# Prompt attention's query, key and value projections: one fp32 product against three f32r products of split operands

## The chip, the cores and the metric

The kernel runs on one core of one Trainium2 chip. The metric is the device time of one execution in microseconds. Each time of the kernel before is from the table below, or from one profiled execution on the same kind of core.

## The reference, cut to what matters

The kernel computes one layer of a hybrid decoder: a recurrence branch, a differential attention branch, a gated merge and a mixture of experts. What concerns us is the attention of the prompt. Its input is `xT`, the normed tokens (1024 channels, 1104 columns: 16 meta tokens, 64 sample tokens, 1024 prompt tokens).

```python
z = rmsnorm(x, norm1_w) @ w_in
hq, hf, hi, hg, dq, dk, dv, ga, gb = split_cols(z)
...
q_b = rmsnorm(dq.reshape(B, T, DA_HEADS, 2, DA_DH), q_norm_w)
k_b = rmsnorm(dk.reshape(B, T, DA_HEADS, 2, DA_DH), k_norm_w)
v_b = dv.reshape(B, T, DA_HEADS, DA_DV)
...
o_b = attn_core(q_b, k_b, v_b, lam)
```

`attn_core` takes per head two softmax maps with a relative bias, subtracts the second times `lam` from the first, and multiplies by the values. All data are float32. `k_b` and `v_b` are outputs too.

## The kernel before

The stages run one behind the other: norm and transposes, recurrence, attention of the prompt, merge (with the attention of the samples inside), output projection and routing, experts. The change lies in the attention stage, `phase_attention`.

That stage works head by head (4), and in each head tile by tile of tokens (9: one of 80 rows, eight of 128). A list of jobs, `slots`, is written out once, and each engine walks through it in its own program. Slot s (head s // 9, tile i = s % 9) has, in this order:

- `z`, the product of tile s+2: 8 steps over the channels, 384 columns (query, key, value of one head), into one PSUM bank (L972);
- `a`, turning the probabilities of slot s-1, one to three groups (L1017);
- the scores of slot s, two maps (L995, L997, in the last tile also L1006);
- `o`, probabilities times values of slot s-1 (L1031);
- `x`, turning query and key of tile s+1 (L981, L982), and `g`, turning the output of slot s-2 (L1039).

The list of one slot, as written:

```python
slot = make[s + AHEAD:s + AHEAD + 1]
...
    slot += [("a", s - 1, g) for g in range(groups(s - 1))]
...
    slot += [("L", s, 0), ("L", s, 1)] + ([("e", s, 0)] if s % NQ == NQ - 1 else [])
```

All jobs but the scores share four PSUM banks in turn (`bank_of`). `bank_free` makes TensorE wait until the job four places back has been read: for a bank that held a product that is the semaphore `normed`, which VectorE raises in `normalise` (L1205). With one group of `a` in a slot the job four places behind `z` is `g`; with two it is `x`; with three it is `o`.

Behind a product, ScalarE copies the values and squares query and key (`square`, L1065 and L1068). VectorE sums the squares (L1195), GpSimd takes the power, and VectorE scales (`normalise`, L1205, L1209). In one slot VectorE's order is: sum of squares, copy of turned probabilities (L928, L930, every second group; ScalarE copies the others at L1104), `maxima` of both maps (L1226, L1238: add the bias in PSUM, then reduce), `normalise`, `combine` (L1248 to L1254), scaling of an output (L1262). ScalarE's exponentials (L1095) stand between them.

Two buffers `Wb` hold the weights of two heads, loaded by SyncE's queue (L939). The keys and values of a head are stored when its last tile is through. Ahead of the first slot stand products 0 and 1 and the turning of tile 0, and the bias rows (L1044, L1122), which go to memory and come back skewed.

The merge stage behind it already multiplies split operands (tile `split`, L1438 to L1440, 368 columns): ScalarE rounds (L1515, L1521), VectorE subtracts the rounded part from the original (L1584, L1588).

Of the kernel before, what the change touches and what calls it, by code (L numbers as in the profile page):

```python
# [24 lines left out]
F32 = mybir.dt.float32  # L25
F32R = mybir.dt.float32r
I32 = mybir.dt.int32
ALU = mybir.AluOpType
# [27 lines left out]
SAMPLE = HEADS * DB * 32 + HEADS * FIRST + HEADS * P + KC * 256 + 2 * HEADS * 256  # L56
OUTPUT_SPLIT = 2 * KC * D + 4 * KC * P
# [78 lines left out]
def build(nc, A, out):  # L136
    with ExitStack() as stack:
# [42 lines left out]
        with nc.sbuf_tensor("sample_part", [P, SAMPLE], F32) as shared:  # L180
# [6 lines left out]
            with nc.sbuf_tensor("attention_part", [P, WORDS - start], F32) as rest:  # L187
                parts.append((rest, start, WORDS - start))
                phase_attention(nc, A, K, out, sb, psum, dram)
                parts.pop()  # L190
# [646 lines left out]
def phase_attention(nc, A, K, out, sb, psum, dram):  # L837

    W = A["w_in"][0].rearrange("(k p) n -> p k n", p=P)
# [33 lines left out]
    with ExitStack() as st:  # L873
        st.enter_context(nc.cleanup_on_exit())
        sem = lambda n: nc.alloc_semaphore(name="attention_" + n)
        w_in = [sem("w_in0"), sem("w_in1")]
# [6 lines left out]
        kv_out = [sem("kv_out0"), sem("kv_out1")]  # L883
# [8 lines left out]
        rel, rel31, relh, bucket, vecs = sb(HEADS), sb(HEADS), sb(HEADS, P), sb(ND), sb(HEADS, ND)  # L892
# [7 lines left out]
        def bank_of(job):  # L900
            return psum[:, 4 + turn_of[job] % 4, :]

# [31 lines left out]
        def _(sp):  # L934
            def weights(h):
                if h >= 2:
                    sp.wait_ge(projected, NT * (h - 1))
                for j, base in enumerate((DQ, DK, DV)):
                    sp.dma_start(Wb[h % 2][:, :, P * j:P * j + P], W[:, :, base + P * h:base + P * h + P]).then_inc(w_in[h % 2], 16)  # L939
# [5 lines left out]
            weights(1)  # L945
# [8 lines left out]
            for h in range(HEADS):  # L954
                sp.wait_ge(x_done, NT * (h + 1))
                for src, big, small in ((kout[h % 2], out["new_k_prompt"], out["new_k_sample"]),
                                        (v[h % 2], out["new_v_prompt"], out["new_v_sample"])):
                    sp.dma_start(big[0, 0, META:, h, :].rearrange("(i p) c -> p i c", p=P), src[:, 1:, :]).then_inc(kv_out[h % 2], 16)
                    sp.dma_start(big[0, 0, 0:META, h, :], src[0:META, 0, :]).then_inc(kv_out[h % 2], 16)
                    sp.dma_start(small[0, :, :, h, :].rearrange("b s c -> (b s) c"), src[META:FIRST, 0, :]).then_inc(kv_out[h % 2], 16)  # L960
                if h + 2 < HEADS:
                    weights(h + 2)
# [1336 lines left out]
```

## Time and profile before

| what | value |
|---|---|
| median of 3 runs | 1724.35 us (1719.77 to 1724.97) |
| the profiled execution's own time | 1728.1 us |
| its span | 1726.3 us |
| TensorE matmuls busy | 1547.2 us, 90% of the span |
| VectorE busy | 707.1 us, 41% |
| ScalarE busy | 461.9 us, 27% |
| GpSimd busy | 235.8 us, 14% |
| mean granted TensorE clock | 0.941 |

The span is the time between the first and the last instruction of the profile; it lies 1.8 us under the execution's own time. [...] An fp32 matmul has two records in the trace, so 8 of them show as x16.

### The profile page before, as it was taken

Reading aid. Unit: us, or ns where it says so; the run is one execution under the profiler, and the core shown is the slowest. Engines: PE = TensorE matmul, PEld = TensorE weight load, DVE = VectorE, ACT = ScalarE, POOL = GpSimd, SP = SyncE. Lnnn points to the kernel's source line nnn. Section 1 sums busy time; section 2 is a strip of 40 time slices with the busy share of each in tenths; the row PEclk is TensorE's granted clock in tenths of the full one; section 3 lists DMA queues with packets and bytes.
Section 4 is the critical chain, followed back from the end, with each engine's and each line's share of the span. In section 5 each row is a group of like instructions: output and inputs, shape, how many; then the busy total and the mean of one; then the engine's idle time right before and its main releaser. Section 6 shows DMA issues by size and latency. Waiting matters only on the chain. (4 is left out here: it accounts for less than half of the span.)

```text
span 1726.3 us, 22053 instructions
## 1 busy us (share of the span) xinstructions
PE 1547.2 (90%) x7497; PEld 1056.2 (61%) x7498; DVE 707.1 (41%) x1465; ACT 461.9 (27%) x1040; POOL 235.8 (14%) x417
## 2 busy tenths in 40 slices
PE   5999999986899898989789999999799929999996
PEld 3566565665465565655568888888678724444442
DVE  4368886886244453444432222233332241222121
ACT  2233343332233343334332222122232200111110
POOL 1000111011222222222100000000000001122221
PEclk8999999987799998989889999999999959999998
DMA  7001200000402001000055667233343392987973
GB/s 243 26 0 59 78 1 26 1 27 1 143 1 63 1 30 35 1 27 1 27 168 183 199 198 251 80 110 110 132 118 110 110 316 76 336 240 227 302 206 49
DMA packets 119369, 186.03 MB, mean 108 GB/s; under 512 B 9507, under 2 KB 82262, under 8 KB 117222
## 3 DMA queue, kind: packets, MB, share of 16 engines
q1 hardware_dynamic: 107750, 134.41, 24.4%
q0 software_dynamic: 11520, 50.34, 10.0%
q8 instruction: 57, 0.93, 0.2%
q14 instruction: 42, 0.34, 0.1%
HBM read 154.38 MB, written 30.34 MB: 107 GB/s over the span
## 5 line engine op out<-in xcount | busy, mean ns | idle before, releaser
L972 PE MATMUL psum<-attention_part,kept 128*128 128x384 f32 (+1 forms) x576 | 205.6, 513 | 0.7 <-DVE attention_part L1205 0.7
L2166 PE MATMUL psum<-moe_part,kept 128*128 x384 | 172.3, 602 | 6.4 <-issue 4.9
L972 PEld LDWEIGHTS psum<-attention_part,kept 128*128 128x128 f32 (+1 forms) x576 | 110.2, 196 | 78.7 <-issue 20.9
L1438 PE MATMUL psum<-split 128*128 128x368 f32 x384 | 140.6, 366 | 2.5 <-DVE split L1584 2.5
L498 PE MATMUL psum<-kept,recurrence_part 128*128 128x368 f32 x384 | 124.7, 480 | 10.0 <-PEq L236 5.0
L1427 PE MATMUL psum<-kept,sample_part 128*128 128x368 f32 x384 | 131.8, 487 | 1.3 <-PEq L873 1.3
L1440 PE MATMUL psum<-split 128*128 128x368 f32 x384 | 127.3, 332 | 0.0
L2166 PEld LDWEIGHTS psum<-moe_part,kept 128*128 128x128 f32 x384 | 72.3, 193 | 89.6 <-issue 89.6
L1439 PE MATMUL psum<-split 128*128 128x368 f32 x384 | 127.0, 331 | 0.0
L503 PE MATMUL psum<-recurrence_part,kept 128*128 128x512 f32 (+1 forms) x288 | 125.9, 593 | 0.0
L1593 DVE TENSOR_TENSOR merge_part<-merge_part,psum 128x368 f32<-128x368 f32 x48 | 25.8, 538 | 220.2 <-ACT merge_part L1527 220.2
L498 PEld LDWEIGHTS psum<-kept,recurrence_part 128*128 128x128 f32 x384 | 72.9, 194 | 54.3 <-issue 7.7
L1427 PEld LDWEIGHTS psum<-kept,sample_part 128*128 128x128 f32 x384 | 71.3, 192 | 41.3 <-issue 7.1
L1527 ACT ACTIVATE merge_part<-psum 128x368 f32<-128x368 f32 x48 | 22.9, 478 | 268.2 <-PE psum L1440 268.2
L503 PEld LDWEIGHTS psum<-recurrence_part,kept 128*128 128x128 f32 (+1 forms) x288 | 52.5, 186 | 64.1 <-issue 64.0
L2153 PE MATMUL psum<-moe_part,kept 128*128 x192 | 86.5, 593 | 1.1 <-ACT kept L2203 1.1
L518 PE MATMUL psum<-recurrence_part 128*128 128x128 f32 (+1 forms) x480 | 65.1, 292 | 21.4 <-DVE recurrence_part L806 21.4
L518 PEld LDWEIGHTS psum<-recurrence_part 128*128 128x128 f32 (+1 forms) x480 | 63.7, 207 | 33.0 <-issue 28.9
L2238 DVE TENSOR_TENSOR kept<-kept,psum 128x256 f32<-128x256 f32 x24 | 10.1, 421 | 168.3 <-ACT kept L2193 168.3
L1438 PEld LDWEIGHTS psum<-split 128*128 128x128 f32 x384 | 72.8, 190 | 9.2 <-DVE split L1584 3.6
L1031 PE MATMUL psum<-attention_part 128*128 128x128 f32 (+2 forms) x360 | 63.1, 321 | 15.7 <-DVE attention_part L1205 14.2
L1439 PEld LDWEIGHTS psum<-split 128*128 128x128 f32 x384 | 72.7, 189 | 5.6
(312 smaller groups left out, 2527.3 us busy)
## 6 DMA issues: line engine op xcount, KB each, us to landing
sample_part<-merge_gates POOLq DMA_DIRECT2D x16, 1024.0 KB
merge_part<-cache_kT SPq DMA_DIRECT2D x64, 256.0 KB, 3.4
merge_part<-cache_v SPq DMA_DIRECT2D x64, 256.0 KB, 3.1
moe_part<-w_gate SPq DMA_DIRECT2D x16, 1024.0 KB, 6.2
moe_part<-w_up SPq DMA_DIRECT2D x16, 1024.0 KB, 12.6
moe_part<-w_down SPq DMA_DIRECT2D x16, 1024.0 KB, 14.0
recurrence_part<-w_in SPq DMA_DIRECT2D x8, 1024.0 KB, 9.2
sample_part<-merge_out POOLq DMA_DIRECT2D x16, 512.0 KB, 6.4
```

What stands on the lines that cost most here:

```text
L498: mm = pe.matmul(bank[:, 0:CH], Wb[0][:, k, c0:c0 + P], K["xT"][:, k, CH * i:CH * i + CH], start=(k == 0), stop=(k == KC - 1))
L503: mm = pe.matmul(bank[:ROWS[i], :], K["xT"][:, k, cols(i)], Wb[1][:, k, :], start=(k == 0), stop=(k == KC - 1))
L518: pe.matmul(lev[:r, l - first, :r], Xu[:, l, xs], Xu[:, l, xs], start=True, stop=True)
L972: mm = pe.matmul(bank_of(("z", h, i))[:ROWS[i], 0:384], K["xT"][:, k, cols(i)], Wb[h % 2][:, k, :], start=(k == 0), stop=(k == KC - 1))
L1031: mm = pe.matmul(bank_of(("o", s, 0))[:r, 0:P], aT[:w, n, :r], v[h % 2][:w, 0 if n == i else n + 1, :], start=(n == 0), stop=(n == i))
L1427: mm = pe.matmul(bank_of(u, 2 * j), Wy[w % 2][:, k, P * j:P * j + P], src[:, k, chunk(n)], start=(k == 0), stop=(k == HEADS - 1))
L1438: pe.matmul(bank_of(u, 2 * j + 1), wh[w % 2][:, k, ch], xh[b][:, k, :], start=(k == 0), stop=False)
L1439: pe.matmul(bank_of(u, 2 * j + 1), wh[w % 2][:, k, ch], xl[b][:, k, :], start=False, stop=False)
L1440: mm = pe.matmul(bank_of(u, 2 * j + 1), wl[w % 2][:, k, ch], xh[b][:, k, :], start=False, stop=(k == KC - 1))
L1593: dve.tensor_tensor(b[:, j, :], b[:, j, :], bank_of(u, 2 * j), ALU.mult).then_inc(mixed, 1)
L2153: mm = pe.matmul(psum[:, 5 + n, :], hT[par][:, k, :], K["Wd"][:, bass.ds(2 * b + k, 1), 512 * n:512 * n + 512], start=(k == 0), stop=(k == 1))
L2166: mm = pe.matmul(psum[:, 2 + par, :], XT[par][:, k, :], K["GU"][:, bass.ds(KC * b + k, 1), :], start=(k == 0), stop=(k == KC - 1))
```

## The change

[...] Each operand is split into a rounded high part and the rest (`xh`, `xl`, `wh`, `wl`, all in a new tensor `attention_split`), and the product is high times high, high times low and low times high: 24 matmuls of 384 columns in place of 8.

```diff
+        view = lambda start, n: split[:, start:start + KC * n].rearrange("p (a b) -> p a b", b=n)
+        wh, wl, xh, xl = view(0, 384), view(KC * 384, 384), view(2 * KC * 384, P), view(2 * KC * 384 + KC * P, P)
-        Wb = [sb(KC, 384) for _ in range(2)]
+        Wb = sb(KC, 384)
...
-        kout = [sb(NT, P) for _ in range(2)]
+        kout = [sb(P) for _ in range(4)]
...
+        start = Pm.rearrange("p a b -> p (a b)")
+        vecs, bucket = start[:, 0:HEADS * ND].rearrange("p (a b) -> p a b", b=ND), start[:, HEADS * ND:HEADS * ND + ND]
+        relh = Am[:, 0:HEADS * P].rearrange("p (a b) -> p a b", b=P)
...
             def weights(h):
-                if h >= 2:
-                    sp.wait_ge(projected, NT * (h - 1))
-                for j, base in enumerate((DQ, DK, DV)):
-                    sp.dma_start(Wb[h % 2][:, :, P * j:P * j + P], W[:, :, base + P * h:base + P * h + P]).then_inc(w_in[h % 2], 16)
+                sp.wait_ge(w_split, 2 * h)
+                sp.dma_start(Wb.rearrange("p a b -> p (a b)"), A["attention_w"][h]).then_inc(w_in, 16)
...
             weights(0)
-            weights(1)
...
+                if h + 1 < HEADS:
+                    weights(h + 1)
+                for i in range(NT):
+                    n = NT * h + i
+                    sp.wait_ge(k_scaled, n + 1)
+                    if i:
+                        sp.dma_start(out["new_k_prompt"][0, 0, META + P * (i - 1):META + P * i, h, :], kout[n % 4]).then_inc(k_out[n % 4], 16)
...
             def product(h, i):
                 bank_free(pe, ("z", h, i))
-                pe.wait_ge(w_in[h % 2], 48 * (h // 2 + 1))
+                pe.wait_ge(x_split, NT * h + i + 1)
+                r, z = ROWS[i], bank_of(("z", h, i))[:ROWS[i], 0:384]
                 for k in range(KC):
-                    mm = pe.matmul(bank_of(("z", h, i))[:ROWS[i], 0:384], K["xT"][:, k, cols(i)], Wb[h % 2][:, k, :],
-                                   start=(k == 0), stop=(k == KC - 1))
+                    if i == 0 and k % 4 == 0:
+                        pe.wait_ge(w_split, 2 * h + k // 4 + 1)
+                    pe.matmul(z, xh[:, k, :r], wh[:, k, :], start=(k == 0), stop=False)
+                    pe.matmul(z, xh[:, k, :r], wl[:, k, :], start=False, stop=False)
+                    mm = pe.matmul(z, xl[:, k, :r], wh[:, k, :], start=False, stop=(k == KC - 1))
                 mm.then_inc(projected, 1)
...
+            def round_next(h, i):
+
+                n = NT * h + i + 1
+                if n < STEPS:
+                    act.wait_ge(projected, n)
+                    if n % NT == 0:
+                        round_w(n // NT)
+                    round_x(n)
+
+            def round_w(h):
+                act.wait_ge(w_in, 16 * h + 16)
+                for g in range(2):
+                    act.activation(wh[:, 4 * g:4 * g + 4, :], Wb[:, 4 * g:4 * g + 4, :], ACT.Copy).then_inc(w_rounded, 1)
+
+            def round_x(n):
+                act.activation(xh[:, :, :ROWS[n % NT]], K["xT"][:, :, cols(n % NT)], ACT.Copy).then_inc(x_rounded, 1)
+
+            round_x(0)
+            round_w(0)
...
                     elif kind == "z":
                         square(a, b)
+                        round_next(a, b)
...
-                if h >= 2:
-                    dve.wait_ge(kv_out[h % 2], 96 * (h // 2))
-                    dve.wait_ge(x_turned, NT * (h - 1))
+                if n >= 4:
+                    dve.wait_ge(k_out[n % 4], k_stored(n - 4))
...
+            def rest_next(h, i):
+                n = NT * h + i + 1
+                if n < STEPS:
+                    if n % NT == 0:
+                        rest_w(n // NT)
+                    rest_x(n)
+
+            def rest_w(h):
+                for g in range(2):
+                    part = slice(4 * g, 4 * g + 4)
+                    dve.wait_ge(w_rounded, 2 * h + g + 1)
+                    dve.tensor_tensor(wl[:, part, :], Wb[:, part, :], wh[:, part, :].bitcast(F32), ALU.subtract).then_inc(w_split, 1)
+
+            def rest_x(n):
+                dve.wait_ge(x_rounded, n + 1)
+                r = ROWS[n % NT]
+                dve.tensor_tensor(xl[:, :, :r], K["xT"][:, :, cols(n % NT)], xh[:, :, :r].bitcast(F32), ALU.subtract).then_inc(x_split, 1)
+
+            rest_x(0)
+            rest_w(0)
...
                     elif kind == "z":
                         sum_squares(a, b)
+                        rest_next(a, b)
```

There is one set of `xh` and `xl`, one of `wh` and `wl` and one `Wb`. To make room, the keys go out tile by tile from a ring of four, and the bias tables lie in the memory of the probabilities. The host lays the weights of one head out in one block (`attention_w`), so that one transfer brings them.

What the change moves on VectorE, in the slot of tile 2 of head 1. The rows before are sum of squares (L1195), the two maxima (L1226, L1238 each), then `normalise` (L1205, L1209):

```order
L1195 TENSOR_REDUCE attention_part<-attention_part 128x4
L1226 TENSOR_TENSOR psum<-psum,attention_part 128x256
L1238 TENSOR_REDUCE attention_part<-psum 128x1
L1226 TENSOR_TENSOR psum<-psum,attention_part 128x256
L1238 TENSOR_REDUCE attention_part<-psum 128x1
L1205 TENSOR_TENSOR attention_part<-psum,attention_part 128x256
```

The same place of the changed kernel, whose lines for these are L1238, L1268, L1280 and L1247; L1335 is the subtraction in `rest_x`:

```order
L1238 TENSOR_REDUCE attention_part<-attention_part 128x4
L1335 TENSOR_TENSOR attention_split<-kept,attention_split 128x1024
L1268 TENSOR_TENSOR psum<-psum,attention_part 128x256
L1280 TENSOR_REDUCE attention_part<-psum 128x1
L1268 TENSOR_TENSOR psum<-psum,attention_part 128x256
L1280 TENSOR_REDUCE attention_part<-psum 128x1
L1247 TENSOR_TENSOR attention_part<-psum,attention_part 128x256
```

One instruction of 1024 elements a partition stands between the sum of squares and the first maximum, and `normalise` follows behind both.

VectorE again, in the slot of tile 6 of head 1, whose product is the last of the head, before:

```order
L1195 TENSOR_REDUCE attention_part<-attention_part 128x4
L928 COPY attention_part<-psum 128x512
L1226 TENSOR_TENSOR psum<-psum,attention_part 128x256
L1238 TENSOR_REDUCE attention_part<-psum 128x1
L1226 TENSOR_TENSOR psum<-psum,attention_part 128x256
```

And in the changed kernel, where L1330 is the subtraction of half the weights of the next head (`rest_w`), and L937 the copy of turned probabilities:

```order
L1238 TENSOR_REDUCE attention_part<-attention_part 128x4
L1330 TENSOR_TENSOR attention_split<-attention_part,attention_split 128x1536 x2
L1335 TENSOR_TENSOR attention_split<-kept,attention_split 128x8x80
L937 COPY attention_part<-psum 128x512
L1268 TENSOR_TENSOR psum<-psum,attention_part 128x256
L1280 TENSOR_REDUCE attention_part<-psum 128x1
```

Two subtractions of weights and a short one of x stand ahead of the copy and the maxima here.

ScalarE at the slot of tile 2 of head 1, before: the values (L1065), the squares (L1068), then at once the exponentials (L1095):

```order
L1065 ACTIVATE attention_part<-psum 128x128
L1068 ACTIVATE attention_part<-psum 128x256
L1095 ACTIVATE attention_part<-psum,attention_part 128x272 x2
L1110 ACTIVATE attention_part<-psum,attention_part 128x128
L1080 ACTIVATE attention_part<-psum,kept 64x128 x2
```

And in the changed kernel, where L1154 is the rounding in `round_x`:

```order
L1084 ACTIVATE attention_part<-psum 128x128
L1087 ACTIVATE attention_part<-psum 128x256
L1154 ACTIVATE attention_split<-kept 128x1024
L1114 ACTIVATE attention_part<-psum,attention_part 128x272 x2
L1129 ACTIVATE attention_part<-psum,attention_part 128x128
```

The rounding stands between the squares and the exponentials.

## Rows read from the trace of the kernel before

**Rows 1.** The page, part 1: busy us (share of the span) x instructions.

```profile
PE 1547.2 (90%) x7497; PEld 1056.2 (61%) x7498; DVE 707.1 (41%) x1465; ACT 461.9 (27%) x1040; POOL 235.8 (14%) x417
```

**Rows 2.** TensorE in order of time, 604.9 to 615.7 us (start, us).

```profile
604.99 5.39 PE L972 MATMUL psum<-attention_part,kept 128*128 128x384 f32 x16
610.21 0.71 PE L1017 MATMUL psum<-kept,attention_part 128*128 128x128 f32 x5
...
615.30 0.30 PE L981 MATMUL psum<-kept,attention_part 128*128 128x128 f32 x1 [0.46 <-DVE attention_part L1205]
...
615.65 0.49 PE L972 MATMUL psum<-attention_part,kept 128*128 128x384 f32 x1
```

**Rows 3.** TensorE's waits, 449 to 830 us: total us, times, longest.

```profile
PE psum L1031 <- DVE attention_part L1205: 14.2, 6, 2.9
PE psum L1039 <- DVE attention_part L1205: 9.4, 15, 1.3
PE psum L981 <- DVE attention_part L1205: 3.8, 10, 0.5
```

**Rows 4.** TensorE in order of time, 581 to 585.65 us.

```profile
582.10 0.38 PE L1017 MATMUL psum<-kept,attention_part 128*128 128x128 f32 x2
...
585.49 0.20 PE L1039 MATMUL psum<-kept,attention_part 16*128 16x16 f32 x1 [0.69 <-DVE attention_part L1205]
```

**Rows 5.** VectorE in order of time, 582.5 to 585.5 us.

```profile
582.88 0.42 DVE L1195 TENSOR_REDUCE attention_part<-attention_part 128x4 f32<-128x256 f32 x1 [3.93 <-ACT attention_part L1068]
583.22 0.42 DVE L1226 TENSOR_TENSOR psum<-psum,attention_part 128x256 f32<-128x256 f32 x1
```

**Rows 6.** VectorE's waits, 449 to 830 us.

```profile
DVE psum L1226 <- PE psum L997: 7.2, 14, 0.7
...
DVE psum L1226 <- PE psum L995: 2.9, 3, 1.0
DVE attention_part L1234 <- PE psum L1006: 1.0, 3, 0.3
```

**Rows 7.** TensorE, 901.4 to 905.3 us: first and last of 23 matmuls.

```profile
901.47 0.33 PE L1439 MATMUL psum<-split 128*128 128x368 f32 x1
...
905.17 0.33 PE L1440 MATMUL psum<-split 128*128 128x368 f32 x1
```

**Rows 8.** VectorE's instructions on tile split: ns min/median/max.

```profile
L1588 DVE TENSOR_TENSOR split<-sample_part,split x16: 2291/2293/2294, 871.1 to 1218.1; 128x2048 fp32r<-128x2048 f32 x16
L1584 DVE TENSOR_TENSOR split<-kept,split x3: 3219/3225/3226, 873.6 to 1128.3; 128x2944 fp32r<-128x2944 f32 x3
```

**Rows 9.** ScalarE's instructions on tile split: ns min/median/max.

```profile
L1521 ACT ACTIVATE split<-sample_part x16: 1901/1902/1911, 869.1 to 1216.1; 128x2048 fp32r<-128x2048 f32 x16
L1515 ACT ACTIVATE split<-kept x3: 2640/2642/2671, 870.9 to 1125.5; 128x2944 fp32r<-128x2944 f32 x3
```

**Rows 10.** TensorE in order of time, 651 to 670.2 us.

```profile
651.75 3.03 PE L1031 MATMUL psum<-attention_part 128*128 128x128 f32 x16 [2.92 <-DVE attention_part L1205]
...
655.24 7.57 PE L972 MATMUL psum<-attention_part,kept 128*128 128x384 f32 x16
...
665.82 3.83 PE L1031 MATMUL psum<-attention_part 128*128 128x128 f32 x18 [1.83 <-DVE attention_part L1205]
```

**Rows 11.** Three stretches (length, busy us by engine, PEclk, DMA share).

```profile
653.00:659.00 6.00, 6.00 (x17) 3.82 (x16) 2.25 (x5) 2.73 (x8) 2.42 (x8) 0.50 0.02 5
667.00:670.00 3.00, 3.00 (x14) 2.55 (x13) 0.00 (x0) 0.27 (x2) 0.00 (x0) 0.50 0.00 0
671.00:700.00 29.00, 26.38 (x106) 16.63 (x105) 12.32 (x38) 11.25 (x41) 6.95 (x17) 1.00 0.00 0
```

**Rows 12.** A longer stretch, 550 to 652 us, the same columns.

```profile
550.00:652.00 102.00, 93.26 (x392) 60.97 (x393) 46.71 (x115) 38.61 (x127) 22.50 (x50) 0.95 0.10 28
```

**Rows 13.** TensorE in order of time, 442 to 456.1 us.

```profile
442.88 13.14 PE L972 MATMUL psum<-attention_part,kept 128*80 128x384 f32 x32
```

**Rows 14.** DMA issues, 425 to 475 us: count, KB each, us to landing.

```profile
attention_part<-w_in SPq DMA_DIRECT2D x6, 512.0 KB, 7.5
```

More of the change, by code:

```diff
@@ L186, in build @@
             assert top[0] == start
-            with nc.sbuf_tensor("attention_part", [P, WORDS - start], F32) as rest:
-                parts.append((rest, start, WORDS - start))
-                phase_attention(nc, A, K, out, sb, psum, dram)
+            with nc.sbuf_tensor("attention_split", [P, ATTENTION_SPLIT], F32R) as split, nc.sbuf_tensor("attention_part", [P, WORDS - start - ATTENTION_SPLIT], F32) as rest:
+                parts.append((rest, start + ATTENTION_SPLIT, WORDS - start - ATTENTION_SPLIT))
+                phase_attention(nc, A, K, out, sb, psum, dram, split)
                 parts.pop()
@@ L834, in _, with phase_attention @@
                     unit_gate(s // 3 + 2)
-def phase_attention(nc, A, K, out, sb, psum, dram):
-    W = A["w_in"][0].rearrange("(k p) n -> p k n", p=P)
+def phase_attention(nc, A, K, out, sb, psum, dram, split):
     NQ = NT
@@ L882, in phase_attention @@
             "logits", "max_done", "exp_done", "a_done", "a_turned", "a_act", "a_dve", "o_done", "ssq_done", "orstd_done", "og_done", "og_turned", "ob_done"))
-        kv_out = [sem("kv_out0"), sem("kv_out1")]
-        Wb = [sb(KC, 384) for _ in range(2)]
+        v_out, k_out = [sem(f"v_out{b}") for b in range(2)], [sem(f"k_out{b}") for b in range(4)]
+        view = lambda start, n: split[:, start:start + KC * n].rearrange("p (a b) -> p a b", b=n)
+        wh, wl, xh, xl = view(0, 384), view(KC * 384, 384), view(2 * KC * 384, P), view(2 * KC * 384 + KC * P, P)
+        Wb = sb(KC, 384)
         qz = [sb(2, TOK) for _ in range(2)]
         kT = [sb(TOK) for _ in range(2)]
-        kout = [sb(NT, P) for _ in range(2)]
+        kout = [sb(P) for _ in range(4)]
         v = [sb(NT, P) for _ in range(2)]
@@ L901, in bank_of, with k_stored @@
             return psum[:, 4 + turn_of[job] % 4, :]
+        def k_stored(n):
+            return 16 * sum(1 + (m % NT == 0) for m in range(n % 4, n + 1, 4))
         def bank_free(e, job):
@@ L981, in turn_qk @@
                 pe.transpose(bank[:, 0:r], zn[:r, n % 2, 0:P], K["ident"][:r, :r])
-                pe.transpose(bank[:, P:P + r], kout[h % 2][:r, i, :], K["ident"][:r, :r]).then_inc(x_turned, 1)
+                pe.transpose(bank[:, P:P + r], kout[n % 4][:r], K["ident"][:r, :r]).then_inc(x_turned, 1)
             def scores(s, m):
@@ L1123, in _ @@
             for kind, a, b in zx:
-                (square if kind == "z" else place_qk)(a, b)
+                if kind == "z":
+                    square(a, b)
+                    round_next(a, b)
+                else:
+                    place_qk(a, b)
             for s, slot in enumerate(slots):
@@ L2291 @@
     arrays["merge_gates"] = np.stack(branch_gate, axis=3).transpose(2, 1, 0, 3, 4).reshape(KC, P, -1).copy()
+    qkv = [arrays["w_in"][0, :, base:base + 512].reshape(KC, P, HEADS, P) for base in (DQ, DK, DV)]
+    arrays["attention_w"] = np.stack(qkv, axis=3).transpose(2, 1, 0, 3, 4).reshape(HEADS, P, -1).copy()
     arrays.update(constants())
```

31 lines of the change are left out of this document (18 added, 13 removed).

## The prediction

> **What bounds the kernel now.** I read the page first, to see whether TensorE is the engine to look at: it is busy 90% of the span [rows 1]. That is an average over stages, so I went to the attention stage (from about 443 us on), laid one slot out in order of time on TensorE, VectorE and ScalarE, and then asked for the waits. I number a slot by its query tile i (0 to 8) within its head, and call T the moment at which its product is over and L1017, the turning of probabilities, starts.
>
> In slot i=5 of head 1 the product starts at 604.99, T is 610.21, and the next product starts at 615.65 [rows 2]. So a product costs 5.22 us, and 5.44 us of other TensorE work and waiting follow. The reader is to see the 0.46 us idle before L981. TensorE there waits for `normed` (L1205), because the bank that it wants next is the one of this slot's product. This wait is not an accident of one slot: L1205 ends 31 waits of TensorE in this stretch, 27.4 us in all [rows 3]. So from T on the slot is set by VectorE's chain: sum of squares, a copy of turned probabilities in some slots, two biased maxima, then `normed`. The 5.22 us of product are set by TensorE. A slot is the sum of the two.
>
> **What the product gains.** The old product is 8 fp32 matmuls of 384 columns in 5.22 us. The new one is 24 matmuls of rounded operands. The same kind runs in the merge stage on 368 columns: from 901.47 to 905.17 there are 22 steps, 0.168 us each [rows 7]. Scaled to 384 columns by 384/368 that is 0.175, so 24 take 4.2 us: **1.04 us less** per product, 36 products, 37 us. A wait on top of it only matters behind these numbers.
>
> [...]
>
> **What the split costs.** Two conversions per product: ScalarE rounds 1024 elements a partition, VectorE subtracts. ScalarE took 1.902 us for 2048 and 2.642 for 2944 [rows 9], so 0.826 ns an element and 1.06 us for 1024. VectorE took 2.293 and 3.225 [rows 8], so 1.04 ns an element and 1.23 us for 1024. For half a head's weights (1536) it is 1.48 and 1.76. Together 57 us on VectorE (33 full x parts, 4 short ones, 8 half weights), 48 us on ScalarE: nothing against their load if it lay under the products. It does not. There is one `xh`, so rounding for product n+1 waits for `projected` of product n, and both engines do it at once, ahead of the slot's copies and maxima (the rows of the order in the section on the change). That is just the chain from T to `normed`.
>
> In time: in slot i=2, T is 582.10, and VectorE's sum of squares starts at 582.88, released by ScalarE's square (L1068), so that ends at about T+0.76 [rows 4, 5]; rounding then ends at T+1.8; the subtraction runs from T+1.84 to T+3.07. Without it VectorE is past its sum of squares at T+1.20 and starts the next work at T+1.12, since its neighbours overlap by some 0.08 [rows 4, 5]. So what follows starts **1.86 us later**. Slot i=2 shows the price bare: VectorE has no gap there, TensorE waits 0.69 us [rows 4], and 0.69 becomes 2.55. Where VectorE now waits for scores ahead of its maxima, that gap takes some of it. All such gaps of the stretch are 7.2 + 2.9 + 1.0 = 11.1 us [rows 6].
>
> The sum, at an unchanged clock:
> - 33 of the 34 slots with a product split for the next one: 33 x 1.86 = 61.4, less the gaps 11.1: **+50.3**.
> - Three of them (i=6 of heads 0 to 2) split the next head's weights first. ScalarE rounds from T+0.7 to T+3.6, VectorE subtracts until T+5.7, then 0.83 for the short x part: what follows starts 3.36 us later than with an x part alone: **+10.1**.
> - 34 products of 1.04: **-35.4**.
> - The opening. The weights of head 0 come at 7.5 us from issue [rows 14], as the first of six issues for two heads, and now in one transfer of 1.5 MB. I take them to be there about 1 us before the old first product began; rounding half of them (1.48) and subtracting it (1.76) then puts the first product near 445, against 442.88 [rows 13]. Products 1 and 2 each wait 3.2 us for their x part where they waited for nothing, and 3 waits 2.8. Against that stand 2 x 1.04, partly at half clock. I take **+8** for it.
> - The K output, now stored tile by tile, and its ring of four: each tile has three slots (about 30 us) to leave, on a queue that carries little here. Put at 0; that it costs under 2 us is bounded by 36 stores of 64 KB behind which only other stores and the next weights stand, and those are issued a head ahead.
> - The aliased bias tables are read before the first slot: 0.
>
> That is +33 us.
>
> **What the longer waits do to the clock.** Twice per head TensorE now idles long enough to be slowed. [...] The product at 655.24 took 7.57 instead of some 5.4. [...] The waits are now 1.83, 1.3, 0.7, 0.7, 0.3, 0.46, 0.4, 0.3 and 2.9 us for i = 0 to 8; with the chain 1.86 us longer less the gaps they become about 3.7, 3.1, 2.6, 2.6, 1.7, 2.1, 5, 1.6 and 3.5. So seven of nine slots are at or above the wait of 1.83 that was followed by a drop. I price a drop by half of its length, as the rows have them: 1.7 us where it lasts 3.4 (i=2, 3, 5), 3.4 where it lasts 6.8 (i=0, 1, 6, 8). That is 18.7 a head against 5.1 now (0.05 of 102 us [rows 12]); heads 1 and 2 lose 13.6 more, head 0 about 8.5, head 3, which has fewer products, 10: **+46** if every such wait brings its drop. Bounds: 0 from below (no more drops than now); from above all products at the lower level, 36 x 4.2 = 150, less the 20 paid now. I take three quarters of the 46, since a slot that runs slow leaves less idle time behind it: **+34**.
>
> So 33 + 34 = 67 us on the profiled execution's 1728.1: 1795. That execution lies 3.75 us (0.2%) over the median of the runs shown, and I forecast **1793 us**, slower by 4%.
>
> **The rivals.**
> - *The chain is longer, the clock as now.* The f32r products keep TensorE warm enough that waits of 2 to 3 us bring no more drops. For it: slot i=1's 1.30 us brought none [rows 3]; against it the 1.83 at 665.82. Time: 1724 + 33 = 1757, range 1745 to 1770. Chance 0.22.
> - *Slow for most of the stage.* Each drop runs into the next wait; the upper bound above, at two thirds: 1724 + 33 + 87 = 1844. For it: two drops lie only some 8 us apart [rows 10, 11]. Chance 0.08.
> - *Faster: the split is hidden.* One mechanism: if what follows `normed` were not waited for, because TensorE reaches its bank wait later than VectorE, the 37 us of products stay and only the opening and the three weight splits (18) are paid: 1724 - 37 + 18 = 1705. It decides from a chain that grows by less than 1.04 us per slot instead of 1.86 less the gaps (1.5 on average). For it: the waits on L981 are short, 0.5 us at most. Against it: they exist in 31 places, so hardly any slack is left on TensorE's side [rows 3]. Chance 0.07.
> - *No change beyond 0.3%*: the chain grows by about 1.2 us per slot and the clock stays. Chance 0.03.
>
> My forecast (chain longer, clock lower more often) has 0.60, with 1772 to 1825 as its own range. The overall range goes down to the first rival's low part and up to 1835, which leaves out the faster cases, the slowest one, and edges: 1748 to 1835. A measurement of this kernel can tell about 0.3% (5 us) from no change. Faster 0.07, same 0.03, slower 0.90.
>
> **What the changed profile would show.** Products: 24 matmuls in 4.2 us at full clock; if they take 5 us, the step of 0.175 is wrong. Rounding 1.06 and subtracting 1.23 us each, ending near T+3.1. TensorE's waits for `normed` in this stretch: 27 us now, near 75 to 90 us then, most of it before the turned output (L1039's line) and before L981's. A mean granted clock of 0.80 to 0.88 between 450 and 830 us, where it is 0.95 in head 1's stretch now [rows 12]; if it stays there, the first rival holds. A wait of 5 us in slot i=6 of heads 0 to 2. The merge stage and later: unchanged. I am wrong if the maxima can start before the subtraction is over, if ScalarE's rounding is much shorter than 1.06 us, or if the lower clock covers mostly the scores, which VectorE's chain hides.

## The result and the profile after

The changed kernel takes **1782.22 us** (median of 4 runs, 1779.48 to 1785.34) where the kernel before takes 1724.66 in the same session (1719.77 to 1726.35): a ratio of 1.0345, interval 1.0319 to 1.037. It is slower by 57.6 us. A few executions took far longer than the others of the same kernel; they are left out of the ratios here. Its profiled execution took 1784.34 us with a span of 1782.5, against 1726.3 before. The span's 56.2 us more lie here: the first product starts 4.4 us later (447.26 against 442.88 [rows 13]), from there to the end of the last product it takes 431.3 us against 382.1 (49.2 more), and what follows takes 2.6 more. Of the 4.4 at the start 2.4 are none of the change's: the bias products ahead of the stage already began that much later.

Part 1 of the page of the changed kernel:

```profile
PE 1547.7 (87%) x7785; PEld 1135.2 (64%) x7786; DVE 760.2 (43%) x1509; ACT 504.6 (28%) x1084; POOL 237.4 (13%) x417
```

VectorE has 53 us more work and ScalarE 43 [rows 1]. TensorE's busy time has not moved, though its products need less of it. The first place to look is again slot i=5 of head 1. TensorE in order of time (start, us):

```profile
634.50 0.41 PE L990 MATMUL psum<-attention_split 128*128 128x384 f32 x1
...
638.77 0.71 PE L1036 MATMUL psum<-kept,attention_part 128*128 128x128 f32 x5
...
642.58 1.54 PE L1050 MATMUL psum<-attention_part 128*128 128x128 f32 x10 [0.59 <-DVE attention_part L937]
645.31 0.30 PE L1000 MATMUL psum<-kept,attention_part 128*128 128x128 f32 x1 [1.19 <-DVE attention_part L1247]
...
645.63 0.41 PE L990 MATMUL psum<-attention_split 128*128 128x384 f32 x1
```

The product is 4.27 us long (638.77 less 634.50) where it was 5.22: 24 float32r matmuls of one record and 0.178 us each in place of 8 of two records and 0.65 us each. These are lengths from start to start; a matmul's own record overlaps the next one's (0.41 us against the step of 0.178). What follows is 6.86 where it was 5.44 [rows 2]. What the product gives, the rest of the slot takes and more. Slot i=2 of head 1 shows by which work. VectorE in order of time; T is 605.02 here:

```profile
605.81 0.42 DVE L1238 TENSOR_REDUCE attention_part<-attention_part 128x4 f32<-128x256 f32 x1 [4.54 <-ACT attention_part L1087]
606.75 1.23 DVE L1335 TENSOR_TENSOR attention_split<-kept,attention_split 128x1024 fp32r<-128x1024 f32 x1 [0.52 <-ACT attention_split L1154]
607.89 0.43 DVE L1268 TENSOR_TENSOR psum<-psum,attention_part 128x256 f32<-128x256 f32 x1
...
609.60 0.41 DVE L1247 TENSOR_TENSOR attention_part<-psum,attention_part 128x256 f32<-128x256 f32 x1
```

The first maximum starts at T+2.87, where it was T+1.12 [rows 4, 5]: 1.75 us later. Before the subtraction VectorE waits for the rounding, 0.52 us. ScalarE in the same slot:

```profile
605.39 0.38 ACT L1087 ACTIVATE attention_part<-psum 128x256 f32<-128x256 f32 x1
605.66 1.06 ACT L1154 ACTIVATE attention_split<-kept 128x1024 fp32r<-128x1024 f32 x1
```

TensorE's waits of the stage, 440 to 900 us (total us, times, longest):

```profile
PE psum L1050 <- DVE attention_part L939: 20.2, 10, 3.2
PE psum L1050 <- DVE attention_part L1247: 19.5, 6, 3.5
PE psum L1058 <- DVE attention_part L1247: 17.2, 15, 2.2
PE psum L1000 <- DVE attention_part L1247: 9.1, 10, 1.2
PE psum L990 <- DVE attention_split L1335: 8.3, 3, 3.0
...
PE psum L1050 <- DVE attention_part L937: 4.6, 3, 3.4
```

L1050, L1058 and L1000 are the outputs, the turned output and the turn of queries and keys, L1031, L1039 and L981 before. L1247 (`normed`) now ends 45.8 us of waits in these three rows where it ended 27.4 [rows 3]. The new rows are L939 and L937, VectorE's copies of the turned probabilities: 24.8 us. They stand behind the subtraction in VectorE's order, and the outputs of the slot need them.

The clock, by two stretches of the profile after (length, busy us by engine, PEclk, DMA share):

```profile
450.00:830.00 380.00, 303.98 (x1506) 261.63 (x1505) 191.26 (x418) 157.69 (x434) 78.03 (x168) 0.87 0.09 29
...
550.00:652.00 102.00, 84.40 (x440) 72.36 (x439) 50.81 (x115) 43.54 (x125) 22.53 (x49) 0.91 0.08 27
```

Over 450 to 830 us the mean granted clock is 0.87 (it was 0.95 in the same stretch before). From the first product to the last, TensorE stood at a granted clock of 0.50 for 115.1 us, against 42.8 before, by the trace's records of that clock, which hold only 1.00 and 0.50; I call this the half-clock time below, and 0.50 the lower level. A product that met the lower level took up to 7.16 us instead of 4.25.

So three things have to be told apart: the shorter product, the longer chain, and the clock.

### The profile page after: what moved, and what is told of

The parts are those of the page before. It is cut to its first block and busy times, and to the rows that moved or that the text cites. A ratio compares the mean times of both kernels' runs of the same rounds, so it can differ in the third digit from the quotient of the medians.

```text
span 1782.5 us, 22725 instructions
## 1 busy us (share of the span) xinstructions
PE 1547.7 (87%) x7785; PEld 1135.2 (64%) x7786; DVE 760.2 (43%) x1509; ACT 504.6 (28%) x1084; POOL 237.4 (13%) x417
## 5 line engine op out<-in xcount | busy, mean ns | idle before, releaser
L990 PE MATMUL psum<-attention_split 128*128 128x384 f32 (+1 forms) x288 | 116.7, 405 | 12.4 <-DVE attention_split L1335 8.3
L991 PE MATMUL psum<-attention_split 128*128 128x384 f32 (+1 forms) x288 | 111.9, 389 | 0.0
L992 PE MATMUL psum<-attention_split 128*128 128x384 f32 (+1 forms) x288 | 111.8, 388 | 0.0
L1050 PE MATMUL psum<-attention_part 128*128 128x128 f32 (+2 forms) x360 | 66.7, 335 | 47.6 <-DVE attention_part L939 20.2
L499 PEld LDWEIGHTS psum<-kept,recurrence_part 128*128 128x128 f32 x384 | 73.1, 194 | 54.5 <-issue 8.1
L1050 PEld LDWEIGHTS psum<-attention_part 128*128 128x128 f32 (+2 forms) x360 | 54.7, 225 | 54.8 <-issue 31.6
```

What stands on the lines that cost most here:

```text
L499: mm = pe.matmul(bank[:, 0:CH], Wb[0][:, k, c0:c0 + P], K["xT"][:, k, CH * i:CH * i + CH], start=(k == 0), stop=(k == KC - 1))
L990: pe.matmul(z, xh[:, k, :r], wh[:, k, :], start=(k == 0), stop=False)
L991: pe.matmul(z, xh[:, k, :r], wl[:, k, :], start=False, stop=False)
L1050: mm = pe.matmul(bank_of(("o", s, 0))[:r, 0:P], aT[:w, n, :r], v[h % 2][:w, 0 if n == i else n + 1, :], start=(n == 0), stop=(n == i))
```

## The experiments

Each session had its own runs of the kernel before, and ratios are against these. Figures of the stage run from the start of the first product to the end of the last.

**1. The splitting of x off the chain.** `xh` and `xl` get a second buffer each, so the parts for tile n+2 can be made at the end of a slot, when both engines have done what TensorE waits for. To make room, the ring of keys and the two work tiles of the norm move into the memory of the merge gates (`Wg_raw`), whose load then starts later. The weights' split stays where it was.

```diff
-        wh, wl, xh, xl = view(0, 384), view(KC * 384, 384), view(2 * KC * 384, P), view(2 * KC * 384 + KC * P, P)
+        wh, wl = view(0, 384), view(KC * 384, 384)
+        xh, xl = ([view(2 * KC * 384 + (2 * b + part) * KC * P, P) for b in range(2)] for part in range(2))
...
                 if 1 <= s <= STEPS:
                     scale_out(s - 1)
+                rest_x(s + 4)
```

> The changed kernel with two sets of xh and xl, so that the x part of tile n+2 is rounded and subtracted at the end of slot n, while TensorE multiplies, and not between projected and the maxima. The weights' split stays where it is. To make room, four small tiles lie in the merge stage's first weight buffer, whose load then comes at the end of the attention stage. My theory (the loss is the x part on VectorE's chain, and the lower clock behind the longer waits): the chain in all slots without a weight split is back to the one before, the products keep 4.25 us, so 1725 - 36 x 1.0 + 3 x 3.6 for the weight splits + 4 for the opening = 1704, within 1697 to 1712, and TensorE's clock in the stage near 0.93. Rival, the three f32r products with their many matmuls are what costs (by the clock or by the operand reads): it stays above 1760.

Measured: **1703.1 us**, ratio 0.9889 (0.9862 to 0.9917): faster than the kernel before by 1.1%, and the theory's 1704 was met. The same work on the same engines, at another place, is worth 79 us. TensorE in slot i=2 of head 1 (T is 568.92; L1061 is the turned output, L1258 `normalise`):

```profile
568.92 0.38 PE L1039 MATMUL psum<-kept,attention_part 128*128 128x128 f32 x2
...
572.31 0.20 PE L1061 MATMUL psum<-kept,attention_part 16*128 16x16 f32 x1 [0.69 <-DVE sample_part L1258]
572.44 0.44 PE L993 MATMUL psum<-attention_split 128*128 128x384 f32 x1
```

The wait is back at the 0.69 us of [rows 4], and half-clock time at 42.3 us.

**2. Only the subtraction behind `normalise`.** VectorE's order alone is changed; there is still one buffer, and ScalarE's rounding stays in its place.

```diff
                     elif kind == "z":
                         sum_squares(a, b)
-                        rest_next(a, b)
...
                 for kind, a, b in slot:
                     if kind == "z":
                         normalise(a, b)
+                        rest_next(a, b)
```

> The changed kernel with one thing moved: on VectorE the subtractions for the next product stand behind normalise of this one, ahead of combine, not ahead of the copies and maxima. Nothing is saved in work. My theory: VectorE no longer waits 0.65 us for ScalarE's rounding and its old gaps ahead of the maxima are used again, but TensorE's next product now waits for the subtraction itself: per head 4 us less, 16 in all, so 1766 (1758 to 1775). Rival, the split's place doesn't matter and only the clock or the products count: 1782 within 5.

Measured: **1776.7 us**, ratio 1.0322 (1.0297 to 1.0347). The theory said 16 us less, 1758 to 1775; the medians are 5.5 us apart, and the interval overlaps that of the changed kernel (1.0319 to 1.037), so the times don't show that anything was won. The waits show what happened. TensorE's, 440 to 900 us:

```profile
PE psum L990 <- DVE attention_split L1335: 49.5, 29, 5.9
PE psum L1050 <- DVE attention_part L1247: 14.0, 6, 2.9
PE psum L1058 <- DVE attention_part L1247: 7.0, 13, 1.0
```

The wait for `normed` is 24.1 us (with 3.1 ahead of L1000), nearly what it was before the change, and the next product waits for the subtraction instead, 29 times. With one buffer the next product cannot start before rounding and subtraction are over, wherever VectorE puts them. Another order around the one buffer moves the wait; the second buffer took it away.

**3. The split with the old product.** The kernel before, with x rounded and subtracted at the changed kernel's places into a result that nobody uses. The product waits for the subtraction as in the changed kernel, but it is the fp32 one.

```diff
                 pe.wait_ge(w_in[h % 2], 48 * (h // 2 + 1))
+                pe.wait_ge(x_split, NT * h + i + 1)
...
                     elif kind == "z":
                         square(a, b)
+                        round_next(a, b)
...
                     elif kind == "z":
                         sum_squares(a, b)
+                        rest_next(a, b)
```

> The kernel before with its fp32 products, and beside them the x part's rounding and subtraction at the very places where the change has them, with the same waits; their result isn't used, and the weights aren't split. My theory: the chain is longer by 1.75 us in 34 slots less some 11 us of gaps, 3 us twice in the opening, and a lower clock behind the longer waits, 10 to 20 us: 1725 + 48 + 6 + 15 = 1794 (1780 to 1810), so slower than the changed kernel although its products are the old ones. Rival, the cost of the change lies in the f32r products, the weights or the stores: 1725 to 1735.

Measured: **1801.69 us**, ratio 1.0473 (1.0437 to 1.0508), within what was expected. The split of x costs 79 us on its own, with no float32r matmul in the kernel. That is more than the whole loss: float32r products, in place of the fp32 ones, bring it down by some 20 us (19.5 between the medians, 21.4 when each is taken against its own session's kernel before), with the weights' split that they need paid from it.

**4. The other edits.** K stored tile by tile from a ring of four, the aliased bias tables and the weights in one block, with fp32 products and no split.

```diff
-        kout = [sb(NT, P) for _ in range(2)]
+        kout = [sb(P) for _ in range(4)]
...
+                sp.dma_start(Wb[h % 2].rearrange("p a b -> p (a b)"), A["attention_w"][h]).then_inc(w_in[h % 2], 16)
```

> The kernel before with the change's other edits alone: keys stored tile by tile from a ring of four, the bias tables in the memory of the probabilities, the weights in one contiguous transfer per head (two buffers kept), and fp32 products without any split. My theory: no effect, 1725 within 5. Rival, the 36 single stores on SyncE's queue or the waits for them cost part of the 57 us: 1735 or more.

Measured: 1722.58 us, ratio 0.9993 (0.9972 to 1.0013). They cost nothing that can be told from zero; the interval allows 2 us more or 5 less.

**5. TensorE kept busy in its waits.** This is to price the clock apart from the chain. Ahead of an instruction that was seen waiting, TensorE runs fp32 products of 128 by 128, about 0.22 us each, into columns of a bank that nobody reads then, counted out per slot to fill 85% of the wait of the trace. Their results are used by nobody. Where that bank isn't free yet, they wait for it first. The other engines' programs are not changed.

```diff
+            def keep_busy(s, kind):
+                n = count[kind][s]
...
+                for _ in range(n):
+                    pe.matmul(bank[:, 384:512], K["xT"][:, 0, 0:P], K["xT"][:, 1, 0:P], start=True, stop=True)
...
                 for kind, a, b in slot:
+                    if kind in "oxg":
+                        keep_busy(s, kind)
                     run[kind](a, b)
```

It was done to the changed kernel:

> The changed kernel with nothing else changed than this: where TensorE stood waiting in the attention slots (ahead of the outputs, of the turns of queries and keys and of the turned output), it first runs fp32 products of 128 by 128 into columns of a bank that nobody reads, 256 of them in all, about 0.22 us each, counted out per slot to fill 85% of the wait that the trace showed there. Their results are used by nobody. Theory (the waits bring the clock down, and the clock costs what the lengthened products cost): time at half clock from the first product to the last falls from 115 us to under 40, products stay at 4.25 us in nearly all slots, and of the 33 us by which 34 products exceed 4.25 us in the changed kernel some 25 go: 1757 us (1745 to 1766). Rival 1 (the falls do not hang on the waits): 115 us at half clock as before, 1782 plus what the added products delay (1782 to 1795). Rival 2 (a product at half clock is hidden by the chain of the other engines): half-clock time goes, the time stays at 1778 to 1784.

to the kernel before:

> The kernel before with the same filling of TensorE's waits, 103 products of 128 by 128. It tells whether the clock has a price in the kernel before too: of 12 us by which its 34 products exceed 5.2 us, some 8 to 10 go: 1716 us (1708 to 1722), half-clock time in the stage from 43 to under 20 us. If the falls do not hang on the waits: 1722 to 1730.

and to the kernel of experiment 1:

> The kernel with two split buffers for x (x_ring_of_two) with the same filling of TensorE's waits, 127 products of 128 by 128. Half-clock time in the stage 42 us to under 20, the excess of 10.6 us in the products mostly gone: 1695 us (1689 to 1702). If the clock has no price there: 1701 to 1706.

| kernel | as it is | waits filled | stage, us | half-clock time, us |
|---|---|---|---|---|
| before | 1724.66 | 1715.73 | 382.1 to 368.0 | 42.8 to 8.9 |
| changed | 1782.22 | 1744.23 | 431.3 to 398.7 | 115.1 to 27.6 |
| ring of two | 1703.1 | 1689.75 | 352.7 to 338.2 | 42.3 to 4.2 |

The ratios to the kernel before are 1.0121 (1.0073 to 1.0168) for the changed kernel with filled waits, 0.9953 (0.9935 to 0.997) for the kernel before with them and 0.9807 (0.9766 to 0.9847) for the ring. The ring and the kernel before came out as expected. With 256 useless products added, the changed kernel is 38 us faster. That is 0.8 us below the range that the theory gave, and neither rival stands: the falls of the clock hang on the waits, and they cost time. Of its 27.6 us of half clock that are left, 20.8 lie in the opening (from the first product to 482.29 us), where only two products were added. Two slots show it. First slot i=8 of head 0 of the changed kernel, TensorE in order of time:

```profile
567.22 3.60 PE L1014 MATMUL psum<-attention_part 128*128 128x512 f32 x8
570.66 0.51 PE L1025 MATMUL psum<-attention_part 128*128 128x16 f32 x4
574.32 2.24 PE L1050 MATMUL psum<-attention_part 128*128 128x128 f32 x16 [3.15 <-DVE attention_part L1247]
```

The same with filled waits, where L1088 are the added products:

```profile
560.23 0.52 PE L1025 MATMUL psum<-attention_part 128*128 128x16 f32 x4
560.59 2.92 PE L1088 MATMUL psum<-kept 128*128 128x128 f32 x24
563.89 2.24 PE L1050 MATMUL psum<-attention_part 128*128 128x128 f32 x16 [0.37 <-DVE attention_part L1270]
```

Twelve products (two records each) fill the wait of 3.15 us down to 0.37, and the outputs start as long after L1025 as before, 3.66 us. The next slot, i=0 of head 1, shows the gain. Its outputs in the changed kernel:

```profile
585.67 4.03 PE L1050 MATMUL psum<-attention_part 128*128 128x128 f32 x18 [3.30 <-DVE attention_part L1247]
```

and with the wait filled:

```profile
572.84 2.94 PE L1088 MATMUL psum<-kept 128*128 128x128 f32 x24 [0.90 <-ACT attention_part L1146]
575.62 2.36 PE L1050 MATMUL psum<-attention_part 128*128 128x128 f32 x18
```

The same 18 records take 2.36 us instead of 4.03. In the changed kernel a stretch at the lower level begins at 586.2 us, inside these outputs. The windows 550 to 652 and 652 to 755 us of the changed kernel with filled waits:

```profile
550.00:652.00 102.00, 97.05 (x605) 84.03 (x606) 58.37 (x125) 47.98 (x136) 23.18 (x50) 1.00 0.08 27
652.00:755.00 103.00, 97.60 (x607) 85.20 (x606) 57.98 (x126) 48.71 (x133) 23.12 (x50) 0.98 0.04 12
```

One blemish: in the kernel before, one wait was overfilled (slot i=8 of head 1, whose next product came at T+12.05 against T+10.13 and T+10.23 in the other heads), so that kernel could be some 1.9 us faster.

**6. Which waits do it.** The same filling of the changed kernel, once in the nine waits of 3.1 to 3.5 us alone, once in all others (2.2 us and less):

> The changed kernel with products of 128 by 128 put only into its nine waits of 3.1 to 3.5 us (ahead of the outputs of i = 6 of the slot loop's turn, i = 8 and the first of the next head, in each head's round), 109 of them. Theory (each fall follows a wait shortly ahead of it, and costs what it lengthens): the falls that stood behind these waits in the changed kernel (at 545.3, 586.2, 657.9, 685.2, 702.3 and 774.0 us, 34 us of half clock in all) go, those of the short slots (from 600, 716 and 815 us on) stay: half-clock time in the stage from 115 to 75 to 90 us, 1767 us (1761 to 1774). Rival (the clock answers to the stage's busy time as a whole): falls thin out everywhere, above all in the short slots too.

> The changed kernel with the products put into the other waits only, of 0.3 to 2.2 us each, 147 of them. By the theory the falls of the short slots go (those that begin at 600, 610, 620, 716, 726, 740, 815, 829, 839 and 849 us), those behind the long waits stay: half-clock time 115 to 50 to 70 us, 1761 us (1755 to 1769). Together the two savings should come near the 38 us that filling all waits gave. Rival (only waits of about 3 us and more bring the clock down, and the short slots' falls are their late echo): half-clock time stays above 100 and the time at 1778 to 1785.

Measured: 1765.29 us (ratio 1.0274, 1.0231 to 1.0318) with the long ones filled, 1758.08 (1.0232, 1.0192 to 1.0271) with the others. The kernel before, run beside these two, took 1718.11 us, 6.5 less than beside the changed kernel, so the medians can't be set against 1782.22 as they stand. Over the kernel before the two are 47.2 and 40.0 us slower, where the changed kernel was 57.6: 10.4 and 17.6 us saved, together 28, against 37.9 with all waits filled. The expectation that the two savings add up to the whole is neither shown nor refuted, as each interval is some 7 us either way. Half-clock time fell to 61.9 and 65.9 us. For the long ones that is more than expected (75 to 90), but part of it is not the added products' doing: in the opening, which has at most two of them, it was 7.4 and 7.9 us, against 26.3 in the changed kernel. (The fall at 815 us, which the expectations count with the short waits, stands behind a wait of 3.30 us.) The products show it slot by slot, from the middle of head 0 into head 1. With the long waits filled, the products of the slots i=2, 3 and 4 of head 1 took 6.70, 5.86 and 6.71 us, and those behind the filled waits of i=8 and i=0 4.26 and 4.34. With the others filled it is the reverse: 4.27, 4.29 and 4.26 in slots i=2 to 4, 6.00 behind the wait in i=6 and 6.30 behind that in i=8. So each kind of wait brings its own falls. With the long ones filled, all but one of the lengthened products behind the opening lie in the slots i=2 to 4. Ahead of each stands a wait of 1.6 to 2.2 us in slot i=1, 2 or 3, one in each slot of 9 to 12 us.

**7. The weights' split off the chain too.** On top of experiment 1, ScalarE rounds the next head's weights behind its copies, and VectorE subtracts behind `normalise`.

```diff
                     elif kind == "z":
                         square(a, b)
+                for kind, a, b in slot:
+                    if kind == "z":
                         round_next(a, b)
                 if s < STEPS:
                     exps(s)
...
                         sum_squares(a, b)
-                        rest_next(a, b)
...
                         normalise(a, b)
+                        rest_next(a, b)
```

> The kernel with two split buffers for x, and the split of the next head's weights taken off the chain as well: ScalarE rounds them after its copy of the turned probabilities and ahead of the exponentials, VectorE subtracts after it has normalised. In the slots of the split (i = 6, three of them, 9.8 us from product to product's start against about 6) first maxima come some 3.5 us sooner; ScalarE's rounding (about 2.8 us) still stands ahead of the exponentials. About 7 us less from the chain and up to 4 from the clock: 1692 us (1687 to 1700). Rival: the rounding delays the exponentials by as much as the subtraction delayed the maxima, so that the slot is as long as it was: 1700 to 1706.

Measured: 1699.6 us, ratio 0.9847 (0.9797 to 0.9897). The three slots i=6 became 12.05 us long in the mean instead of 14.1, 6 us in all, but the interval overlaps that of the ring, 0.9862 to 0.9917, so the times don't tell it. The same with TensorE's waits filled as well:

> Two split buffers for x, the weights' split off the chain, and TensorE's waits filled with 106 products. The ring with filled waits took 1689.8 us; taking the weights' split off the chain made three slots 1.7 us shorter each in the trace: 1685 us (1679 to 1691). Rival (the weights' split gives nothing more, since VectorE's subtraction then delays the next product): 1688 to 1692.

Measured: 1682.7 and 1683.3 us, with no ratio from so few, so the same kernel ran again:

> The kernel of ring_weights_kept_busy once more (88 added products, not the 106 that its expectation gave), since only two of its four executions were undisturbed, at 1682.7 and 1683.3 us. 1683 us (1680 to 1689), which puts it 5 to 7 us below the ring with filled waits and the weights' split left on the chain, and 2.0 to 2.4% below the kernel before. If the two executions were a lucky draw of the clock: 1687 to 1692.

Measured: **1685.0 us** (1682.92 to 1686.8, 6 runs), ratio 0.9778 (0.9753 to 0.9803), against 0.9807 (0.9766 to 0.9847) for the ring with filled waits. It is the fastest version found, 2.2% below the kernel before. That the weights' part of it is a gain is not shown by the times here either, since the intervals overlap; what shows it is the length of the three slots. What is left of the weights' split is in the waits of the first of these two runs, 440 to 785 us:

```profile
PE psum L993 <- DVE attention_split L1365: 5.2, 4, 1.5
PE psum L1061 <- DVE sample_part L1283: 3.3, 13, 0.4
```

L993 belongs to the product, L1365 is the subtraction of weights: the first product of each of the three next heads waits 1.5 us, in place of the 3.5 us by which the split had delayed `normed` (`normalise` of slot i=6 ended at T+9.07 in heads 0 and 2 of the ring, now at T+5.60).

## Why the prediction was right, and where its terms were off

The forecast was +69 us on the median, the measured change is +57.6, in the range and in the likeliest case: the chain longer and the clock lower. Its steps in their order:

- **The product, 1.04 us less.** Measured 4.24 to 4.27 against 5.22 at the full clock, 0.96 less, 32.7 us for 34 products at full clock against the 35.4 of the sum. The step measured on 368 columns held nearly: 24 steps from 634.50 to 638.77 are 0.178 us each, where 0.175 was forecast.
- **What follows starts 1.86 us later.** Measured 1.75, and 1.06 and 1.23 us for the two conversions as forecast. The start of the subtraction (T+1.73 against T+1.84) is what was off.
- **The gaps, and +50.3.** With the waits filled in both kernels, so that the clock hardly speaks, the 28 slots from the third on that split no weights are 37 us longer outside their products (the overfilled one set right), 1.32 each; the sum had 1.52. In slots i=1 to 3 the 1.75 came through nearly whole (1.5 to 1.9), in i=7 it was 0.6 to 0.7 and in i=8 0.2 to 0.3. There VectorE waited 0.65 to 0.72 and 0.94 to 0.99 us for scores ahead of its maxima in the kernel before, and part of the subtraction fell into that time; the rest of the difference is not traced. Only in these slots, and barely in i=5 of heads 0 and 2 (0.93 and 0.96), does the rival "faster: the split is hidden" hold, since there the chain grew by no more than the 0.96 that the product gives; over all slots it does not.
- **The weights' split, three slots.** 4.50, 4.34 and 4.37 us longer outside the product, 13.2 in all; the sum had 3 x (3.36 + 1.52) = 14.6.
- **The opening, +8.** The first product came 2.0 us later by the change's own doing, and products 1, 2 and 3 waited 3.03, 2.80 and 2.51 us: 10.3, less 1.9 for two shorter products, 8.4. The weights were there at 443.8 us, 6.9 from issue, not 1 us before the old first product; the stage had begun 2.4 us later too.
- **The K stores and the aliases, 0.** Experiment 4 shows it to within 5 us.
- **The clock, +34.** Without its falls the change would cost 1744.23 less 1715.73, 28.5 us, where the sum had 33. The rest of the 57.6, **29 us**, goes away when the waits are filled in both kernels. But not all of it can be put down to the waits of the stage. By the four profiled executions the difference is 29.9 us, and only 18.5 of it lie in the stage (32.6 less 14.1). The other 11 lie ahead of the stage and behind it, where no product was added: there the changed kernel was 5.2 and 3.7 us shorter in its filled version, the kernel before 0.2 and 2.2 longer. So the clock's price is 18.5 us as the traces of the stage have it, 29 as the medians have it. The cause was right; the size was 5 us too large by the medians and 15 by the traces. The lengths in the price, 3.4 and 6.8 us, are those of the two falls per head in the trace of the kernel before (666.6 to 670.0 and 652.9 to 659.7 us in head 1, at 0.50). Seven of nine waits were forecast at or above the 1.83 that was followed by a fall [rows 10, 11], and falls did come at waits of that size (1.6 to 2.2 us in experiment 6). Not each wait brought one, though: behind the 3.15 us in slot i=8 of heads 0 and 2, priced at 3.4 us each, the next product took 4.27.
- **The forecast of the waits for `normed`**, 75 to 90 us: the step that failed. They are 45.8. The prediction followed VectorE's chain to `normed` alone, and put the copies of turned probabilities into it as a link only. They are waited for themselves: the outputs need them, they come ahead of the maxima, and they stand right behind the subtraction. In slot i=6 of head 0 TensorE waited 3.21 us for one of them. Both kinds together are 70.6 us, 4 below the range; that was a forecast near in the sum and wrong in what is late. Of the 45.8 themselves, 26.3 stand where they were expected most, before the turned output and the turn of queries and keys, and 19.5 before the outputs. That this did not move the predicted time I explain by both kinds of waits having the same cause, the subtraction ahead of them; no run tests it alone.
- **The mean clock**, 0.80 to 0.88 between 450 and 830 us: 0.87.
- **The wait of 5 us in slots i=6**: it came in pieces, 3.2 to 3.4 us for the copy in all three heads, and in heads 0 and 1 another 0.3 and 0.6 for `normed`. TensorE had the outputs still to do between them.
- **Slips in the working.** There are 32 full x parts and four short ones, not 33; the 57 and 48 us of work are right for 32. And 67 us on the median give 1791, not 1793. Neither matters here.

What stays open is the price of the clock's falls between 18.5 and 29 us. Half-clock time outside the stage moved too: ahead of it 62.4 us in the changed kernel's profile and 50.9 in that of its filled version, behind it 107.5 and 93.7. Why, no run tells. The intervals of the ratios alone leave the 29 us uncertain by nearly 10 either way.

## What to carry to other kernels

A conversion that feeds the next step costs its duration only if it stands between a result and somebody who waits for it; the split of x took 79 us more ahead of the maxima than at the end of the slot (1782.22 against 1703.1 us). Before placing it, list what is queued behind it on its engine and who waits for each of these, and if a single buffer forces the place, buy the second buffer; reordering around one buffer only moved the wait here (1776.7 us, against 1782.22 as it was and 1703.1 with the second buffer). Where such waits come in every slot, count what they cost in slowed matmuls behind them as well: here 18 to 29 us, beside some 59 for the chain itself, from which the shorter products gave back 33. Matmuls whose results are thrown away won most of the clock's part back: 256 of them brought 1782.22 us down to 1744.23.

## What the runs showed of the hardware

- With only the long waits filled, TensorE still fell to a granted clock of 0.50 in slots whose waits were 1.6 to 2.2 us (61.9 us of half-clock time in the stage, 54.5 of it behind the opening). With all waits filled the mean clock was 1.00 from 550 to 652 us and 0.98 from 652 to 755, where it had been 0.91 and 0.83.
- The kernel before, with its TensorE 90% busy, had a price of the clock too: 8.8 us came back when 103 products filled its waits (1724.57 us in that session, 1715.73 filled).
- A wait of about 3 us was not followed by a fall each time: behind the 3.15 us in slot i=8 of head 0 (574.32) the clock stayed up until 586.2.
- The added products did not delay the waiting instruction where they were counted out under the wait: the outputs of slot i=8 started 3.66 us after L1025 in both kernels (570.66 to 574.32, 560.23 to 563.89).
